# Query, key and value products as three rounded products of split weights and split latents, in a two-layer hybrid backbone on one core

## The chip, the cores and the metric

One Trainium2 chip, of which the kernel uses one core. The time is that of one execution on the device, in microseconds (us); the median of several runs counts. The core has five engines that run side by side and wait for each other by semaphores: TensorE (PE in the profile, its weight loads PEld), VectorE (DVE), ScalarE (ACT), GpSimd (POOL) and SyncE (SP), whose queue issues the weight transfers.

## The reference

Two trunk layers over 128 context tokens and 256 latent tokens, 384 in all, model width 1024, everything in fp32. Cut to what matters here:

```python
h = rms_norm(x, norm1) * (1 + scale1) + shift1
conv_in, q_lat, kv_lat, k_rope, gates = split_projection(h @ w_in)   # 1024 | 256 | 128 | 32 | 2048 wide
conv_out = conv_module(conv_in, ...)      # a * sigmoid(b), depthwise conv of width 31, LayerNorm, silu, pointwise
q   = rms_norm((rms_norm(q_lat, q_lora_norm) @ w_uq).reshape(.., 8, 96), q_norm)
ckv = rms_norm(kv_lat, kv_lora_norm)
k_nope, v = split((ckv @ w_ukv).reshape(.., 8, 64 + 64))
k   = rms_norm(concat(k_nope, k_rope), k_norm)
# latent tokens: rotary on q and k, and keys and values of 128 cached tokens are appended
att = softmax(q @ k.T * 96 ** -0.5) @ v @ w_o
x   = x + gate1 * ((sigmoid(g_conv) * conv_out + sigmoid(g_att) * att) @ w_out)
x   = x + gate2 * hier_moe(rms_norm(x, norm2) * (1 + scale2) + shift2)
```

Outputs are x of both groups, and ckv and k_rope of the context tokens for each layer.

## The kernel before, in words

**Weights.** All weights come as units of 128 x 2048 fp32 (1 MB) into a ring of six slots, one after the other on SP's queue. A load waits until the unit that was in its slot six units earlier has been used. Units of one kind, `raw_unit`, are multiplied as they lie, as fp32, by `product` (L849). Others are **split** first: `make_hi` on ScalarE copies the unit into `w_hi` in the type float32r, which rounds it (the **top**, L725), and `make_lo` on VectorE subtracts the top from the unit into `w_lo` (the **rest**, L731). `split_product` (L862) then makes three rounded products, top x top, top x rest and rest x top, into the same PSUM bank. The slot is free once the rest is made; the place of top and rest is free once TensorE has gone on to its next product. Before the gates there are three places, for the gate units two, in turn. The split units stand in `SPLIT` and are numbered in the order of use; `hi(n)` and `lo(n)` in the engines' programs make top and rest of the n-th.

**Order.** Each engine has a program that is written out by hand; nothing is scheduled. For a layer the order around the change is:

1. The norm of x; the latent products (queries' latent, keys' and values' latent, rotary key: 416 columns for each of three token tiles) and glu unit 0, interleaved. The tokens `h` are split as well.
2. ScalarE squares the three latent tiles in PSUM with accumulation (L1553), takes roots (L1555, L1556), VectorE inverts them (L1939) and scales the latents out of PSUM into `cq`, `ckv` and `kr` (L1942 to L1944). ScalarE meanwhile goes on to the sigmoid of glu unit 0 (L1561), which needs another activation table.
3. Glu units 0 to 3. For each, ScalarE makes a sigmoid and the top of the unit two further on, and VectorE multiplies into `u` (L1980, L1981), adds taps of the convolution into `z` and makes the rest of that unit. One **tap** is one instruction over 128 x 399 elements (L1967); there are 4 x 31 in a layer. `CONV_GLU` and `CONV_GATES` say how many stand after each glu and gate unit. After glu unit 2 (`LATT_AFTER`), TensorE turns `cq` and `ckv` (L840), and VectorE multiplies the turned latents by the norm's gain into `cqT` and `ckvT` (L1989) and copies the cached latent behind them (L1984).
4. Queries: six half tiles of 384 columns, two chunks of 128 in depth each, raw. Keys and values: four tiles of 512 columns each, one chunk, raw. ScalarE squares every tile of queries and keys into one of two halves of `scratch` (L1575, L1583) and copies tile and values out of PSUM; VectorE reduces the squares (L2016, L2023), with one tap behind each reduction. A square waits until the reduction two before it is done.
5. Gate units 0 to 7, each with two halves of 384 columns x 8 chunks (48 matmuls), and between them units of the conditioning projection (`ada`, L873, 16 matmuls): one after each gate unit in layer 0 (two after the last), and one after every second in layer 1. In step c VectorE does its part of the norm and the rotary of queries and keys (`steps`), `CONV_GATES[c]` taps, and then a rest; ScalarE makes a sigmoid of both halves and then a top. Ahead of gate unit 7 TensorE turns the queries.
6. When all taps are done, TensorE multiplies `z` with ones for the mean of the LayerNorm (L849, 128 x 399, the **mean product**), and the keys are turned. Attention, output products and the experts (MoE) follow.

The lookahead of the gates: the rests of gate units 0 and 1 are made after glu units 2 and 3, that of gate unit c + 2 at the end of step c.

## Time and profile before

| what | value |
|---|---|
| median of 3 runs | 939.18 us (937.98 to 943.5) |
| the profiled execution | 938.33 us, of which 936.5 us is the span from first to last instruction |
| busy: PE, DVE, ACT, POOL | 903.0, 749.6, 494.5, 34.9 us |
| chain that ended last | PE 77%, DVE 14%, ACT 3%, DMA 2% |
| raw fp32 products in it | PE ps L849, 7% of the span |
| rest of a full unit, DVE L731 | 40 in 91.5 us, 2288 ns each |
| top of a full unit, ACT L725 | 44 in 84.0 us, 1909 ns each |
| granted TensorE clock | 0.994 |

The span is the time between the first and the last instruction of the profiled core; the profiled execution's own time is 1.8 us longer. Busy time is a sum over stages, so it does not say which engine is late in one. Instructions on one engine overlap at their ends: for what one costs in a row of its kind, the distance between starts is read, not its duration. The chain of waits goes back from the last instruction to whatever released each one, so an engine named there is the one that was late.

### The profile page before, as it was taken

The numbers are of one execution on the slowest core, as the hardware profiler recorded it, in microseconds if no ns is written. First come the engines' busy times: TensorE is split into PE (matmuls) and PEld (weight loads), VectorE is DVE, ScalarE is ACT, GpSimd is POOL, SyncE is SP. The second block draws the span as 40 slices with busy tenths as digits, with TensorE's granted clock in tenths as the row PEclk, the third lists the DMA queues.
The fourth block names the chain that finished last, engine by engine and source line by source line (L and its number), as shares of the span: only waits on it lengthen the run. The fifth ranks groups of instructions, "written<-read, shape, count | busy, mean of one in ns | idle before, by whom it ended". The sixth has DMA issues, their size and how long they took to land.

```text
span 936.5 us, 14465 instructions
## 1 busy us (share of the span) xinstructions
PE 903.0 (96%) x5486; PEld 759.1 (81%) x5486; DVE 749.6 (80%) x1263; ACT 494.5 (53%) x704; POOL 34.9 (4%) x60
## 2 busy tenths in 40 slices
PE   4999999999999999999999999999999999999998
PEld 3897898768888778887868969996699878888886
DVE  4589899768754899779966998996798479986995
ACT  4345522567322687647754363336653267864872
POOL 1000000040000000000000000001400000000000
PEclk9999999999999999999999999999999999999999
DMA  9953665412464799849939336431152168993971
GB/s 369 421 203 139 232 251 192 180 46 90 185 244 170 286 373 362 329 142 387 377 124 363 129 108 270 171 135 46 46 178 95 44 235 326 374 371 132 351 278 68
DMA packets 29014, 206.54 MB, mean 221 GB/s; under 512 B 3408, under 2 KB 3440, under 8 KB 4240
## 3 DMA queue, kind: packets, MB, share of 16 engines
q1 hardware_dynamic: 28656, 204.81, 57.2%
q8 instruction: 44, 0.72, 0.3%
q0 software_dynamic: 288, 0.79, 0.2%
q14 instruction: 26, 0.21, 0.1%
HBM read 203.85 MB, written 1.74 MB: 220 GB/s over the span
## 4 chain that ended last, share of the span: by engine, by line
PE 77%; DVE 14%; ACT 3%; issue 2%; DMA 2%; SPq 0%; DVEq 0%; ACTq 0%
PE ps L862 57%; PE ps L849 7%; DVE z L1967 4%; PE ps L873 3%; DVE w_lo L731 3%; PE ps L840 2%; DMA ring<-wpre 2%; PE ps L1323 2%; ACT kT L1604 1%; PE ps L1420 1%; PE ps L1421 1%; PE ps L1146 1%; ACT w_hi L725 1%; PE ps L1134 1%; DVE w_lo L736 1%
## 5 line engine op out<-in xcount | busy, mean ns | idle before, releaser
L736 DVE TENSOR_TENSOR w_lo<-ring,w_hi 128x2048 fp32r<-128x2048 f32 (+2 forms) x104 | 227.4, 2197 | 16.1 <-ACT w_hi L1714 15.0
L862 PE MATMUL ps<-h_hi,w_hi 128*128 128x384 f32 x576 | 198.7, 345 | 1.7 <-DVE x L2212 0.6
L862 PE MATMUL ps<-h_hi,w_lo 128*128 128x384 f32 x576 | 193.6, 336 | 0.0
L862 PE MATMUL ps<-h_lo,w_hi 128*128 128x384 f32 x576 | 193.4, 336 | 0.0
L1714 ACT ACTIVATE w_hi<-ring 128x2048 fp32r<-128x2048 f32 x96 | 182.7, 1914 | 12.8 <-PE ps L862 12.5
L1967 DVE SCALAR_TENSOR_TENSOR z<-u,par,z 128x399 f32<-128x399 f32 x240 | 137.2, 630 | 1.4
L862 PEld LDWEIGHTS ps<-h_hi,w_hi 128*128 128x128 f32 x576 | 108.1, 188 | 14.3 <-issue 8.6
L731 DVE TENSOR_TENSOR w_lo<-ring,w_hi 128x2048 fp32r<-128x2048 f32 x40 | 91.5, 2288 | 27.7 <-ACT w_hi L725 27.7
L862 PEld LDWEIGHTS ps<-h_lo,w_hi 128*128 128x128 f32 x576 | 108.2, 188 | 0.5 <-issue 0.5
L862 PEld LDWEIGHTS ps<-h_hi,w_lo 128*128 128x128 f32 x576 | 108.1, 188 | 0.0
L862 PE MATMUL ps<-w_hi,hg_hi 128*128 128x512 f32 x256 | 103.3, 404 | 1.5 <-DVE hg_lo L736 1.5
L725 ACT ACTIVATE w_hi<-ring 128x2048 fp32r<-128x2048 f32 x44 | 84.0, 1909 | 32.4 <-DMA ring<-wpre 16.9
L862 PE MATMUL ps<-w_hi,hg_lo 128*128 128x512 f32 x256 | 100.6, 393 | 0.0
L862 PE MATMUL ps<-w_lo,hg_hi 128*128 128x512 f32 x256 | 100.5, 393 | 0.0
L1598 ACT ACTIVATE gates<-ps 128x384 f32<-128x384 f32 x32 | 15.7, 491 | 95.6 <-PE ps L862 95.5
L862 PEld LDWEIGHTS ps<-w_hi,hg_hi 128*128 128x128 f32 x256 | 48.1, 188 | 11.4 <-issue 1.9
L862 PEld LDWEIGHTS ps<-w_hi,hg_lo 128*128 128x128 f32 x256 | 48.1, 188 | 10.9
L862 PEld LDWEIGHTS ps<-w_lo,hg_hi 128*128 128x128 f32 x256 | 48.2, 188 | 9.3
L862 PE MATMUL ps<-w_hi,hT_hi 128*128 128x512 f32 x128 | 51.5, 402 | 0.3
L873 PE MATMUL ps<-ring,condp 128*32 128x256 f32 x768 | 51.3, 395 | 0.2 <-DMA ring<-wpre 0.2
L862 PE MATMUL ps<-w_lo,hT_hi 128*128 128x512 f32 x128 | 50.5, 395 | 0.0
L862 PE MATMUL ps<-w_hi,hT_lo 128*128 128x512 f32 x128 | 50.3, 393 | 0.0
(267 smaller groups left out, 1359.1 us busy)
## 6 DMA issues: line engine op xcount, KB each, us to landing
ring<-wpre SPq DMA_DIRECT2D x96, 1024.0 KB, 6.9
ring<-wmoe SPq DMA_DIRECT2D x96, 1024.0 KB, 6.7
x<-x SPq DMA_DIRECT2D x1, 1536.0 KB, 7.6
x_out<-x SPq DMA_DIRECT2D x4, 384.0 KB, 2.3
par<-par_in POOLq DMA_DIRECT2D x2, 304.5 KB, 7.1
const<-const_in SPq DMA_DIRECT2D x1, 314.0 KB, 2.8
ckv_out<-ckvT POOLq DMA_DIRECT2D x2, 64.0 KB, 5.3
kr_out<-kr POOLq DMA_DIRECT2D x2, 16.0 KB, 5.8
```

The lines of the kernel that those rows point to most:

```text
L725: nc.scalar.activation(w_hi[place_of(n)], slot(pre_slot(l, at)), ACT.Copy).then_inc(split_hi, 1)
L731: nc.vector.tensor_tensor(w_lo[place_of(n)], slot(pre_slot(l, PRE_AT[l][SPLIT[n]])), w_hi[place_of(n)].bitcast(F32), ALU.subtract).then_in ...
L736: return nc.vector.tensor_tensor(out, whole, leading.bitcast(F32), ALU.subtract)
L840: m = nc.tensor.transpose(out[:, n * P:(n + 1) * P], src, ident)
L849: m = mm(out, lhs[i], rhs[i], start=(i == 0), stop=(i == n - 1))
L862: m = mm(out, a, b, start=(start and i == 0 and j == 0), stop=(stop and i == n - 1 and j == 2))
L873: m = mm(ps[32 * j:32 * j + 32, ADA_BANK, 0:ADA_COLS], condp[:, 2 * j + c, at:at + 32], w[:, 2 * j + c, :], start=(u == 0 and c == 0), sto ...
L1134: m = nc.tensor.transpose(out[:, b * P:(b + 1) * P], probs[i % PROBS][:, b * P:(b + 1) * P], ident)
L1323: m = mm(out, src[:, t, f * P:(f + 1) * P], pick[:, t, :], start=(opens and c + t + part == 0), stop=(closes and c + t + part == 1 + TT))
L1598: af(gates[:, c, :], ps_of("gate", c)[:, 0:TOK], ACT.Sigmoid).then_inc(taken["act"], 1)
L1714: af(w_hi[m % MOE_PLACES], slot(moe_slot(l, m)), ACT.Copy).then_inc(split_hi, 1)
L1967: m = stt(z[:, c, :], src, dw[:, c, tap:tap + 1], z[:, c, :], ALU.mult, ALU.add)
```

## The change

The query unit `uq` and the key-value unit `ukv` become split units (1536 and 1024 of 2048 columns are converted). The turned latents are split as well, into `cqT_hi`, `cqT_lo`, `ckvT_hi`, `ckvT_lo`, which lie where the gates are written later. TensorE makes three rounded products for each of the former raw ones. With two more split units, `SPLIT` numbers gate unit 0 as 8 where it was 6. ScalarE scales the raw latents, in place of VectorE, and takes the latent banks. Six taps that stood one behind each query reduction now stand behind the last gate unit, which has 21 for 15.

```diff
-SPLIT = [e for e in PRE[0] if e[0] in ("lat", "glu", "gate", "wo", "pw2", "wout")]
+SPLIT = [e for e in PRE[0] if e[0] in ("lat", "glu", "uq", "ukv", "gate", "wo", "pw2", "wout")]
...
+def unit_width(n):
+    return {"uq": 2 * H * QK, "ukv": H * (NOPE + VD)}.get(SPLIT[n][0], UNIT)
...
-CONV_GATES = [12, 8, 11, 8, 10, 5, 15, 15]
+CONV_GATES = [12, 8, 11, 8, 10, 5, 15, 21]
...
@@ TensorE @@
-                w = raw_unit("uq", 0)
+                w = split_unit("uq", 0, 2, H * QK)
...
-                    product(out[:, 0:n], [cqT[:, c, t * P:(t + 1) * P] for c in range(2)],
-                            [w[:, c * H * QK + half * n:c * H * QK + (half + 1) * n] for c in range(2)]
-                            ).then_inc(psum_full, 1)
-                held.append(raw_used)
-                w = raw_unit("ukv", 0)
+                    split_product(out[:, 0:n], pairs(cqT_hi, cqT_lo, 2, t * P, (t + 1) * P), w(half * n, (half + 1) * n)
+                                  ).then_inc(psum_full, 1)
+                held.append(split_used)
+                w = split_unit("ukv", 0, 1, H * (NOPE + VD))
                 for t in range(KT):
+                    if t == KT - 1:
+                        pe.wait_ge(cache_split, l + 1)
...
-                        product(out[:, 0:512], [ckvT[:, t * P:(t + 1) * P]], [w[:, half * 512:(half + 1) * 512]]
-                                ).then_inc(psum_full, 1)
-                held.append(raw_used)
+                        split_product(out[:, 0:512], [(ckvT_hi[:, t * P:(t + 1) * P], ckvT_lo[:, t * P:(t + 1) * P])],
+                                      w(half * 512, (half + 1) * 512)).then_inc(psum_full, 1)
+                held.append(split_used)
@@ ScalarE @@
+                act.wait_ge(lat_inverted, l + 1)
+                for t in range(TT):
+                    src = ps_of("lat", t)
+                    af(cq[:, t, :], src[:, 0:QL], ACT.Identity, scale=lat_r[:, t:t + 1])
+                    af(ckv[:, t, :], src[:, QL:QL + KVL], ACT.Identity, scale=lat_r[:, 3 + t:4 + t])
+                    af(kr[:, t, :], src[:, QL + KVL:QL + KVL + ROPE], ACT.Copy).then_inc(taken["act"], 1)
                 for c in range(KC):
...
+                    if c == LATT_AFTER:
+                        for n in range(3):
+                            wait_full(act, l, "latT", n)
+                            src = ps_of("latT", n)[:, 0:TOK]
+                            if n < 2:
+                                af(cqT_hi[:, n, :], src, ACT.Identity, scale=pf("q_lora")[:, n:n + 1]).then_inc(lat_hi_done, 1)
+                            else:
+                                af(ckvT, src[:, 0:CTX], ACT.Identity, scale=pf("kv_lora"))
+                                af(ckvT_hi[:, TOK:KEYS], pf("cache_ckv"), ACT.Copy)
+                                af(ckvT_hi[:, 0:TOK], src, ACT.Identity, scale=pf("kv_lora")).then_inc(lat_hi_done, 1)
...
+                hi(8)
                 for t in range(KT):
...
+                hi(9)
                 act.wait_ge(head_summed, l + 1)
...
-                    if c % 2 and 8 + c // 2 < EARLY_SPLITS:
-                        hi(8 + c // 2)
+                    if c % 2 and 10 + c // 2 < EARLY_SPLITS:
+                        hi(10 + c // 2)
@@ VectorE @@
-                chain(nc.vector.reciprocal(lat_r, lat_r))
-                for t in range(TT):
-                    src = ps_of("lat", t)
-                    vs(cq[:, t, :], src[:, 0:QL], lat_r[:, t:t + 1], None, ALU.mult)
-                    vs(ckv[:, t, :], src[:, QL:QL + KVL], lat_r[:, 3 + t:4 + t], None, ALU.mult)
-                    copy(kr[:, t, :], src[:, QL + KVL:QL + KVL + ROPE]).then_inc(taken["dve"], 1)
+                nc.vector.reciprocal(lat_r, lat_r).then_inc(lat_inverted, 1)
...
                     if c == LATT_AFTER:
-                        mark(copy(ckvT[:, TOK:KEYS], pf("cache_ckv")))
+                        conv_taps(c + 1, LATT_TAPS)
                         for n in range(3):
-                            wait_full(dve, l, "latT", n)
+                            dve.wait_ge(lat_hi_done, l * 3 + (n + 1))
                             part = pf("q_lora")[:, n:n + 1] if n < 2 else pf("kv_lora")
-                            dst = cqT[:, n, :] if n < 2 else ckvT[:, 0:TOK]
-                            vs(dst, ps_of("latT", n)[:, 0:TOK], part, None, ALU.mult).then_inc(taken["dve"], 1)
-                    conv_taps(c + 1, CONV_GLU[c])
+                            dst, top = (cqT_lo[:, n, :], cqT_hi[:, n, :]) if n < 2 else (ckvT_lo[:, 0:TOK], ckvT_hi[:, 0:TOK])
+                            stt(dst, ps_of("latT", n)[:, 0:TOK], part, top.bitcast(F32), ALU.mult, ALU.subtract
+                                ).then_inc(taken["dve"], 1)
+                        lower(ckvT_lo[:, TOK:KEYS], pf("cache_ckv"), ckvT_hi[:, TOK:KEYS]).then_inc(cache_split, 1)
+                    conv_taps(c + 1, CONV_GLU[c] - (LATT_TAPS if c == LATT_AFTER else 0))
                     lo(4 + c)
...
-                    conv_taps(KC, 1)
+                lo(8)
                 for t in range(KT):
...
-                    if 8 + c < EARLY_SPLITS:
-                        lo(8 + c)
+                    if 9 + c < EARLY_SPLITS:
+                        lo(9 + c)
```

Three places of the programs, before and after. In these rows `w_hi_85`, `w_hi_86` and `w_hi_89` are the three places of tops, `w_lo_87`, `w_lo_88` and `w_lo_90` those of rests. The lines of the changed kernel have other numbers.

ScalarE between the roots of the latent norm and the sigmoid of glu unit 0, before:

```order
L1555 ACTIVATE small<-small,eps 128x3
L1556 ACTIVATE small<-small,eps 128x3
L1561 ACT_TABLE_LOAD
L1561 ACTIVATE sig<-ps 128x384
L725 ACTIVATE w_hi_86<-ring 128x2048
```

and in the changed kernel:

```order
L1573 ACTIVATE small<-small,eps 128x3
L1577 ACTIVATE cq<-ps,small 128x256
L1578 ACTIVATE ckv<-ps,small 128x128
L1579 ACTIVATE kr<-ps 128x32
L1577 ACTIVATE cq<-ps,small 128x256
L1578 ACTIVATE ckv<-ps,small 128x128
L1579 ACTIVATE kr<-ps 128x32
L1577 ACTIVATE cq<-ps,small 128x256
L1578 ACTIVATE ckv<-ps,small 128x128
L1579 ACTIVATE kr<-ps 128x32
L1584 ACT_TABLE_LOAD
L1584 ACTIVATE sig<-ps 128x384
```

Nine instructions came to stand between the roots and the table load; the first of them waits for VectorE's reciprocal.

VectorE from the last key reductions into the gate steps, before (the rest of gate units 0 and 1 is made ahead of this piece; `w_lo_87` here is that of unit 2, `w_lo_88` that of unit 3):

```order
L2023 TENSOR_REDUCE small<-scratch 128x8
L1967 SCALAR_TENSOR_TENSOR z<-u,par,z 128x399
L2029 TENSOR_TENSOR small<-small 128x32
L1967 SCALAR_TENSOR_TENSOR z<-u,par,z 128x399 x12
L731 TENSOR_TENSOR w_lo_87<-ring,w_hi_85 128x2048
L2034 RECIPROCAL small<-small 128x56
L2036 TENSOR_TENSOR q<-q,small 128x768 x3
L1967 SCALAR_TENSOR_TENSOR z<-u,par,z 128x399 x8
L731 TENSOR_TENSOR w_lo_88<-ring,w_hi_86 128x2048
```

and in the changed kernel, where the first row is the rest of gate unit 0 and the last that of gate unit 1:

```order
L747 TENSOR_TENSOR w_lo_87<-ring,w_hi_85 128x2048
L2055 TENSOR_REDUCE small<-scratch 128x8
L1997 SCALAR_TENSOR_TENSOR z<-u,par,z 128x399
L2055 TENSOR_REDUCE small<-scratch 128x8
L1997 SCALAR_TENSOR_TENSOR z<-u,par,z 128x399
L2055 TENSOR_REDUCE small<-scratch 128x8
L1997 SCALAR_TENSOR_TENSOR z<-u,par,z 128x399
L2055 TENSOR_REDUCE small<-scratch 128x8
L1997 SCALAR_TENSOR_TENSOR z<-u,par,z 128x399
L2061 TENSOR_TENSOR small<-small 128x32
L1997 SCALAR_TENSOR_TENSOR z<-u,par,z 128x399 x12
L747 TENSOR_TENSOR w_lo_88<-ring,w_hi_86 128x2048
```

Each gate unit's rest has moved one gate step nearer to its use.

ScalarE between queries and keys, before:

```order
L1575 ACTIVATE scratch<-ps 128x384
L1576 ACTIVATE q<-ps 128x384
L1583 ACTIVATE scratch<-ps 128x512
L1584 ACTIVATE k<-ps 128x8x64
L1587 ACTIVATE v<-ps 128x512
```

and in the changed kernel:

```order
L1608 ACTIVATE scratch<-ps 128x384
L1609 ACTIVATE q<-ps 128x384
L740 ACTIVATE w_hi_85<-ring 128x2048
L1617 ACTIVATE scratch<-ps 128x512
L1618 ACTIVATE k<-ps 128x8x64
L1621 ACTIVATE v<-ps 128x512
```

The top of gate unit 0, which stood before the queries, now stands between queries and keys; that of gate unit 1 stands behind the last values.

## Rows read from the trace of the kernel before

**Rows 1.** The page, part 1: busy us, share of the span, instructions.

```profile
PE 903.0 (96%) x5486; PEld 759.1 (81%) x5486; DVE 749.6 (80%) x1263; ACT 494.5 (53%) x704; POOL 34.9 (4%) x60
```

**Rows 2.** The chain of waits, layer 1, from 533 to 575: start, us, what.

```profile
543.91 1.00 PE ps L873 x16
544.91 14.80 PE ps L849 x40
559.72 8.50 PE ps L862 x48
...
568.63 1.91 ACT w_hi L725
```

**Rows 3.** The chain of waits, layer 1, from 605 to 640.

```profile
618.64 16.37 DVE z L1967 x30
...
635.15 2.93 PE ps L849 x8
```

**Rows 4.** The chain of waits over the whole span, layer 0.

```profile
61.38 8.53 PE ps L862 x48
...
81.43 14.80 PE ps L849 x40
96.23 8.38 PE ps L862 x48
...
162.74 2.76 PE ps L840 x24
...
175.75 2.89 PE ps L849 x8
```

**Rows 5.** Timeline of DVE, layer 0: start, us, engine, line, operation.

```profile
51.97 0.19 DVE L1939 RECIPROCAL small<-small 128x6 f32<-128x6 f32 x1 [2.55 <-ACT small L1556]
...
54.53 0.29 DVE L1980 TENSOR_TENSOR u<-ps,sig 128x128 f32<-128x128 f32 x1
...
58.93 2.29 DVE L731 TENSOR_TENSOR w_lo<-ring,w_hi 128x2048 fp32r<-128x2048 f32 x1
```

**Rows 6.** Timeline of ACT, layer 0, latent norm and first sigmoid.

```profile
50.26 0.42 ACT L1553 ACTIVATE unused<-ps 128x256 f32<-128x256 f32 x1
...
51.04 0.29 ACT L1554 ACTIVATE unused<-par 128x32 f32<-128x32 f32 x1
...
51.95 1.28 ACT L1561 ACT_TABLE_LOAD   x1
53.25 0.49 ACT L1561 ACTIVATE sig<-ps 128x384 f32<-128x384 f32 x1
53.63 1.91 ACT L725 ACTIVATE w_hi<-ring 128x2048 fp32r<-128x2048 f32 x1
```

**Rows 7.** Timeline of ACT, layer 0, keys and the turned queries.

```profile
91.32 0.60 ACT L1583 ACTIVATE scratch<-ps 128x512 f32<-128x512 f32 x1
...
97.33 1.28 ACT L1590 ACT_TABLE_LOAD   x1
...
163.24 3.85 ACT L1596 ACTIVATE qT<-ps,par 96x384 f32<-96x384 f32 x8 [0.97 <-PE ps L840]
```

**Rows 8.** Timeline of DVE, layer 0, reductions and the taps behind them.

```profile
86.66 0.55 DVE L2016 TENSOR_REDUCE small<-scratch 128x4 f32<-128x384 f32 x1
...
96.36 0.69 DVE L2023 TENSOR_REDUCE small<-scratch 128x8 f32<-128x512 f32 x1 [0.17 <-ACT scratch L1583]
...
97.61 6.63 DVE L1967 SCALAR_TENSOR_TENSOR z<-u,par,z 128x399 f32<-128x399 f32 x12
```

**Rows 9.** Timeline of DVE, layer 1, the first gate steps.

```profile
570.57 2.29 DVE L731 TENSOR_TENSOR w_lo<-ring,w_hi 128x2048 fp32r<-128x2048 f32 x1 [2.85 <-ACT w_hi L725]
572.78 0.49 DVE L2034 RECIPROCAL small<-small 128x56 f32<-128x56 f32 x1
...
582.48 0.95 DVE L2042 TENSOR_TENSOR q<-q,par 128x768 f32<-128x768 f32 x1
```

**Rows 10.** The page, part 6: transfers, KB each, median us from issue to landing.

```profile
ring<-wpre SPq DMA_DIRECT2D x96, 1024.0 KB, 6.9
```

More of the change, by code:

```diff
@@ L222 @@
 LATT_AFTER = 2
+LATT_TAPS = 4
 HROW_EARLY = 5
@@ L286, in pre_jobs @@
     for t in range(TT):
-        add("lat", t, "dve", 4 + t)
+        add("lat", t, "act", 4 + t)
     for c in range(KC):
@@ L463, in build @@
         probsT_at = work_at + 4 * 3 * TOK
-        cqT = v3(place("cqT", 2 * TOK, at=probsT_at), 2)
         ckvT_at = probsT_at + 4 * 2 * TOK
-        ckvT = place("ckvT", KEYS, at=ckvT_at)
+        cqT_hi = v3(place("cqT_hi", 2 * TOK, F32R, at=gates_at), 2)
+        cqT_lo = v3(place("cqT_lo", 2 * TOK, F32R, at=gates_at + 4 * 2 * TOK), 2)
+        ckvT_hi = place("ckvT_hi", KEYS, F32R, at=gates_at + 4 * 4 * TOK)
+        ckvT_lo = place("ckvT_lo", KEYS, F32R, at=gates_at + 4 * (4 * TOK + KEYS))
+        assert 4 * TOK + 2 * KEYS <= KD * TOK
+        ckvT = place("ckvT", CTX, at=ckvT_at)
         scratch_at = ckvT_at + 4 * KEYS
@@ L615, in build @@
         lat_rms = sem("lat_rms")
+        lat_inverted = sem("lat_inverted")
+        lat_hi_done = sem("lat_hi_done")
+        cache_split = sem("cache_split")
         squared = sem("squared")
@@ L724, in make_hi @@
                 eng.wait_ge(split_used, base + (earlier[-1] + 1))
-            nc.scalar.activation(w_hi[place_of(n)], slot(pre_slot(l, at)), ACT.Copy).then_inc(split_hi, 1)
+            used = unit_width(n)
+            nc.scalar.activation(w_hi[place_of(n)][:, 0:used], slot(pre_slot(l, at))[:, 0:used], ACT.Copy).then_inc(split_hi, 1)
         def make_lo(eng, l, base, n):
             eng.wait_ge(split_hi, base + (n + 1))
-            nc.vector.tensor_tensor(w_lo[place_of(n)], slot(pre_slot(l, PRE_AT[l][SPLIT[n]])),
-                                    w_hi[place_of(n)].bitcast(F32), ALU.subtract).then_inc(split_lo, 1)
+            used = unit_width(n)
+            nc.vector.tensor_tensor(w_lo[place_of(n)][:, 0:used], slot(pre_slot(l, PRE_AT[l][SPLIT[n]]))[:, 0:used],
+                                    w_hi[place_of(n)][:, 0:used].bitcast(F32), ALU.subtract).then_inc(split_lo, 1)
         def lower(out, whole, leading):
@@ L811, in _ @@
                 wait_taken(pool, l, "latT", 2)
-                pool.dma_start(ckv_out[l], ckvT[:, 0:CTX]).then_inc(ckv_stored, 16)
+                pool.dma_start(ckv_out[l], ckvT).then_inc(ckv_stored, 16)
                 pool.dma_start(kr_out[l], kr[:, 0, :]).then_inc(ckv_stored, 16)
```

## The prediction, made before the result was known

> **What bounds the kernel now.** I read the page first: TensorE is busy for 96% of the span [rows 1], an average over stages with different limits. So I went to the chain of waits in the second layer, where queries, keys and values are made. There it runs through TensorE alone: the first products on whole fp32 numbers (40 matmuls, 14.80 us), then gate unit 0 (8.50), and then leaves it: ScalarE makes the top of gate unit 2, VectorE its rest, and from there it stays on VectorE [rows 2] up to the last 30 convolution taps, which end at 635.0; the mean product starts at 635.15 [rows 3]. So what bounds the gate stage is VectorE in layer 1, and TensorE in layer 0, where the chain goes from the gates straight to the mean product at 175.75 [rows 4]. A saving on TensorE before the gates counts only if VectorE, which makes the rest of every weight unit, is there as early.
>
> Write T for the start of the first query product: 81.43 before in layer 0, 544.91 in layer 1 [rows 4, 2].
>
> **Step 1, the products: a gain on TensorE.** A 384-column rounded product costs 8.50/48 = 0.177 us [rows 2]; one of 512 columns I scale to 0.236. Queries: 6 half tiles x 2 chunks x 3 = 36, 6.4 us. Keys and values: 8 x 3 = 24, 5.7 us. Together 12.0 (14.8 if short products gained nothing), against 14.80: **2.8 us less** of TensorE per layer.
>
> **Step 2, the latents move to ScalarE: a loss.** Before, ScalarE loaded the sigmoid table at 51.95 while VectorE did the nine scalings, between its reciprocal (51.97) and the gating product at 54.53 [rows 5, 6]. Afterwards the scalings come ahead of the table load, and VectorE can do nothing in between but one small copy. Price: a token tile of three ACTIVATEs took 51.04 - 50.26 = 0.78 with three accumulator reads of 0.09, so 0.51 without [rows 6]; the two scaled ones carry a per-partition scale, and eight such 384-wide ones took 3.85, 0.47 each, against 0.38 between the starts at 53.25 and 53.63 [rows 6, 7], so 0.09 more: 0.68 a tile, 2.05 in all (bounds 1.5 and VectorE's own 2.3). With reciprocal and hand-overs, 0.25, the sigmoid ends 2.3 later, at 56.05, and VectorE goes on at 56.1 instead of 54.53: **1.5 late** (bounds 1.0 and 1.8). Nothing absorbs it: the rest of glu unit 2 ended at 58.93 + 2.29 = 61.22 and TensorE took it at 61.38, after ready work up to about 61.3 [rows 5, 4]. So TensorE starts glu unit 2 1.4 late in layer 0 and 1.5 in layer 1, and T becomes 82.85 and 546.4.
>
> The table load took 1.28 us and the sigmoid began 1.30 after its start [rows 6]. The Trainium skill (ScalarE: Activation LUTs, What ACT_TABLE_LOAD costs) adds a drain of some 1.38 us to every switch. By that rule, with the load now uncovered, each layer would lose 1.4 more; by the row, nothing. The trace disagrees with the rule here, so it is a small rival below.
>
> **Step 3, six more latent instructions.** ScalarE makes the tops of the turned latents after the query weights' top (about 1.8 us); VectorE meanwhile has four taps (2.4), so it should find them ready. Its own three rests replace three scalings. Cost nothing while those taps cover it; without them up to 1.8. Query and key-value weights are split at 3/4 and 1/2 of a 2.20 us unit, in the places where gate units 0 and 1 were split. All needed units were asked for long before: the queries' by the release of glu unit 1's slot, the others by TensorE's first product of glu unit 2 and the end of its rest.
>
> **Step 4, from T to gate unit 1: the decisive wait.** Before, VectorE began the first reduction at 86.66, T + 5.2 [rows 8]. Now the split before it is half as long (-1.1) and the gating product need not wait for a full-size split (-0.45): T + 3.7. ScalarE then goes at its own pace, since no tap stands between reductions: third square at T + 4.3, four queries x 0.77, done at T + 7.4. Now comes the new top of gate unit 0 (1.91 [rows 6]), T + 9.35; then four key/value tiles, 97.33 - 91.32 = 6.0 [rows 7]. VectorE makes gate unit 0's rest (2.2), T + 11.55, then four reductions (0.60 apart from the tap, 0.55 each tap), T + 16.2. Before it was at 97.61 - 81.43 = T + 16.2 too [rows 8]: **VectorE has been relieved of six taps and of half a split, and yet is no earlier, because ScalarE's order holds it**. Then twelve taps (6.6 us for 12 [rows 8]) and only then the rest of gate unit 1, T + 22.8 to T + 25.1. ScalarE's top of it (T + 15.4 to 17.3) is no limit.
>
> TensorE wants it at T + 12.0 + 8.5 (gate unit 0) + 1.0 (one conditioning unit in layer 0 only [rows 2]): T + 21.5 and T + 20.5. Before, gate units 0 and 1 had both been split before the reductions, and the twelve taps stood ahead of unit 2. So there is a new wait of TensorE: **3.7 us in layer 0, 4.7 in layer 1**. It eats the gain of step 1 whole: a TensorE that gained nothing would merely wait 2.8 less.
>
> Behind it in the queues: ScalarE's top of gate unit 2 waits for TensorE to leave unit 0 (over by then); VectorE's next things, reciprocals and query scaling, wait for roots that are long there.
>
> **Step 5, the gates.** In **layer 0** TensorE needs 9.5 a unit, VectorE's first step after it 582.48 - 572.78 = 9.7 [rows 9], so 0.2 more is lost, and from there VectorE gains on it (15 taps and a split, 10.4, stand against a gate, a conditioning unit and the 2.76 of transposes [rows 4]). The six moved taps end at about 175.9 and the mean product comes at 178.2: they are hidden. Sum: 1.4 - 2.8 + 3.7 + 0.2 = **+2.5**.
>
> In **layer 1** VectorE sets the end. It has the rest of unit 1 done at 546.4 + 25.2 = 571.6. Then, as before from 572.78 to 618.64, five steps: 45.85; then 15 taps (16.37/30 each, 8.2), one more split (2.2) and 21 taps (11.45) [rows 3, 9]: 639.3, mean product 639.45 against 635.15. TensorE would be there at 571.6 + 7 x 8.5 + 4 x 1.0 + 2.8 = 637.9. Cross-check: the work behind its wait of 2.85 at 570.57 [rows 9] grew by a split and six taps, 5.5, less that wait, plus 1.5 of step 2: **+4.2 to +4.3**. Here the six taps (3.3) are paid in full.
>
> After the mean product nothing is moved; the waits there are on the same engines in the same order, so I carry both shifts to the end.
>
> **The sum.** 2.5 + 4.3 = 6.8 us. Profiled execution 938.33 (span 936.5 and 1.8 around it): 945.1. The median of the runs, 939.18, is 0.85 above it: **946.0**.
>
> **Rivals.** (A) *Faster:* VectorE gets to gate unit 1 before TensorE, so the new wait is not there. It takes 3.7 and 4.7 us; the reductions would have to follow TensorE's key products (T + 12) and not ScalarE. Then TensorE keeps its gain: layer 0 1.4 - 2.8 = -1.4, layer 1 4.3 - 4.7 = -0.4: 939.2 - 1.8 = 937.4. For it: VectorE lost six taps from this stretch. Against: ScalarE's 1.91 us in the middle of it. Half of it (2.5 us earlier) gives 941. Chance 0.12.
> (B) *Slower:* squares and reductions take turns instead of overlapping (two scratch halves, and no tap to fill): 0.49 + 0.55 + 0.2 against 0.77, for four queries 1.9 a layer. Both ends hang on VectorE's time at gate unit 1, so all of it is paid: 946.0 + 3.8 = 949.8. It decides once a square waits for the reduction just before it. Chance 0.12.
> (C) The drain, per layer 1.4: 948.8. Chance 0.04.
> (D) The ring: gate units' slots come free a step later, and SP's queue holds all loads behind them. In layer 0 gate unit 4's load then begins at 108, when gate unit 1 is split, for use after 126, and a load takes 6.9 in the median [rows 10]. If it did bite in each gate, 950 to 960. Chance 0.04.
> (E) The products gain nothing: the time is the forecast's, as said.
>
> **Numbers.** The forecast 0.68. The range takes in (A)'s half, the bounds of steps 2 and 4 (about 1 us a layer each) and (B): 940 to 950.5. About 1% (9.4 us) is what a measurement can tell: faster than 929.8 needs more than the whole gain of TensorE with no loss, 0.02; slower than 948.6 holds most of (B), (C), (D) and the forecast's edge, 0.16; within 0.82.
>
> **What would show it.** Sigmoid of glu unit 0 about 2.3 after its old time; glu unit 2's products released by VectorE's rest, 1.4 late; query to value products 12.0 long; gate unit 1's first matmul waiting 3.7 and 4.7 us for VectorE's split, which follows twelve taps; the mean product at about 178.2 and 639.4; in layer 0 TensorE late there, in layer 1 VectorE. It is wrong if gate unit 1 does not wait, or if the later stages give any of it back.

## The result, and the profile after

| | before | after |
|---|---|---|
| median of the runs, us | 941.34 (937.98 to 944.21, 4 runs) | 952.39 (952.0 to 954.96, 4 runs) |
| ratio, with its 95% interval | | 1.0126 (1.0098 to 1.0154) |
| profiled execution, us | 938.33 | 952.0 |
| span, granted TensorE clock | 936.5, 0.994 | 950.2, 0.983 |

The kernel became slower by 1.3%. The forecast was 946.0 with a range up to 950.5; between the two profiled executions it had +6.8 us, and +13.7 was measured.

The page of after: part 1 (busy us of each engine), and from part 2 the granted clock in 40 slices.

```profile
PE 905.8 (95%) x5526; PEld 772.1 (81%) x5526; DVE 751.0 (79%) x1249; ACT 506.6 (53%) x736; POOL 35.0 (4%) x60
...
PEclk9999999999999999999999998999999979999999
```

TensorE is busy 2.8 us longer than in [rows 1], though its products got shorter. Busy time contains whatever runs at a lower clock, so this alone says that the clock has to be looked at.

The view of waits, engine PE, of after: line, whom it waited for, us in total, times, longest.

```profile
PE ps L878 <- DVE w_lo L747: 12.3, 5, 4.7
```

Before, the rest of a unit (then L731) held TensorE for 0.2 us in all. So the change made a wait of TensorE for VectorE's rests, 12.1 us more of it. Some of it takes the place of work saved, so it isn't yet a loss.

ScalarE's timeline of after, layer 0: the last latent copy, the table load, the sigmoid of glu unit 0 (start, us).

```profile
54.00 0.25 ACT L1579 ACTIVATE kr<-ps 128x32 f32<-128x32 f32 x1
54.27 1.28 ACT L1584 ACT_TABLE_LOAD   x1
55.56 0.49 ACT L1584 ACTIVATE sig<-ps 128x384 f32<-128x384 f32 x1
```

The sigmoid starts at 55.56 where it started at 53.25 [rows 6]: 2.31 later, as forecast. The load still took 1.28, and the sigmoid began 1.29 after its start. Now the load has nothing to hide behind, and there is still no drain beside it.

The chain of waits of after, whole span, read at the places of the prediction (start, us, what):

```profile
62.93 8.59 PE ps L878 x48
...
83.05 6.68 PE ps L878 x37
...
99.47 6.54 DVE z L1997 x12
106.01 2.21 DVE w_lo L747
108.27 10.27 PE ps L878 x48
...
180.14 2.89 PE ps L865 x8
...
490.23 1.11 PE ps L989 x8
...
530.78 10.16 PE ps L878 x48
...
575.42 2.21 DVE w_lo L747
577.68 11.20 PE ps L878 x48
...
646.04 2.89 PE ps L865 x8
...
783.58 5.77 PE ps L878 x24
```

The order of events is the predicted one: glu unit 2 behind the rest at 62.93; T = 83.05; twelve taps, then gate unit 1's rest, which ends at 108.22 = T + 25.2, and in layer 1 at 577.63 = T + 25.2 too. What was not predicted is the length of the row behind each wait. A gate or glu unit of 48 matmuls took 8.4 to 8.5 us in layer 0 of before [rows 4], and glu unit 2 of its layer 1 8.60; these three take 10.27, 10.16 and 11.20. TensorE's own timeline of after shows why (in brackets how long it sat idle before, and for what):

```profile
62.93 0.44 PE L878 MATMUL ps<-h_hi,w_hi 128*128 128x384 f32 x1 [1.74 <-DVE w_lo L747]
...
108.27 0.44 PE L878 MATMUL ps<-h_hi,w_hi 128*128 128x384 f32 x1 [3.65 <-DVE w_lo L747]
...
530.78 0.44 PE L878 MATMUL ps<-h_hi,w_hi 128*128 128x384 f32 x1 [1.94 <-DVE w_lo L747]
...
577.68 0.69 PE L878 MATMUL ps<-h_hi,w_hi 128*128 128x384 f32 x1 [4.75 <-DVE w_lo L747]
578.16 0.52 PE L878 MATMUL ps<-h_lo,w_hi 128*128 128x384 f32 x1
578.48 0.52 PE L878 MATMUL ps<-h_hi,w_lo 128*128 128x384 f32 x1
...
584.00 0.34 PE L878 MATMUL ps<-h_hi,w_hi 128*128 128x384 f32 x1
584.18 0.34 PE L878 MATMUL ps<-h_lo,w_hi 128*128 128x384 f32 x1
...
770.26 3.64 PE L889 MATMUL ps<-ring,condp 128*32 128x256 f32 x32
```

The waits are 3.65 us at gate unit 1 in layer 0 and 4.75 in layer 1, for 3.7 and 4.7 forecast. Behind the latter the matmuls start 0.32 apart, and by 584 0.18 apart. The granted clock was at its lower level (1.2 of 2.4 GHz, here called half clock) for 6.8 us there, from 576.3 on, that is from within the wait. Behind the wait of 1.74 at 62.93 it did not fall (8.59 us for the 48), behind that of 1.94 at 530.78 it did. The last row lies at the head of layer 1's experts, behind no long wait: 32 matmuls of a conditioning unit. TensorE's timeline of before has the same 32:

```profile
758.41 1.93 PE L873 MATMUL ps<-ring,condp 128*32 128x256 f32 x32
```

The view of windows of after (bounds, us, busy of PE, PEld, DVE, ACT, POOL, granted clock, DMA share, GB/s) shows the same:

```profile
100.00:120.00 20.00, 16.35 (x104) 14.61 (x103) 19.97 (x30) 7.92 (x11) 0.00 (x0) 0.91 0.28 106
520.00:540.00 20.00, 18.06 (x106) 17.16 (x105) 15.06 (x22) 7.96 (x14) 0.00 (x0) 0.91 0.29 106
560.00:580.00 20.00, 15.26 (x75) 13.92 (x74) 18.34 (x28) 15.25 (x22) 0.00 (x0) 0.91 0.31 107
760.00:780.00 20.00, 18.53 (x150) 13.42 (x150) 12.45 (x56) 9.99 (x13) 0.00 (x0) 0.74 0.52 197
```

The same view of before:

```profile
100.00:120.00 20.00, 20.00 (x135) 18.34 (x134) 17.00 (x23) 6.72 (x8) 0.00 (x0) 1.00 0.73 281
300.00:320.00 20.00, 17.80 (x170) 14.42 (x160) 16.24 (x60) 11.14 (x17) 0.59 (x1) 0.91 0.66 256
740.00:760.00 20.00, 20.00 (x161) 15.36 (x159) 10.43 (x45) 6.18 (x13) 0.00 (x0) 0.91 0.15 54
```

Before, the gate stages ran at 1.00, and the lower level came at the start (20), at the very end (935) and at the head of the experts, in both layers (0.91, one stretch of 3.4 us each, at 303 and at 754). After, there are further stretches behind the new waits (109, 532, 576.3). At the head of the experts it is 3.4 us again in layer 0 (317), but 10.2 us in layer 1 (764 to 774).

What TensorE did just before 754 in the kernel before is not a wait. Its timeline:

```profile
753.48 0.82 PE L1271 MATMUL ps<-par,xa 128*128 128x20 f32 x6
754.14 2.09 PE L840 MATMUL ps<-const,xa 128*128 128x128 f32 x9
```

The clock fell at 754.2, at the end of 28 matmuls of only 20 columns or 1 column that had run without a gap from 751.0 on. In layer 0 it fell at 303.5, near the end of the same 28. The short waits of this stage (0.55 us at 760.89 and 0.92 at 762.45) come later. In layer 1 of after it fell at 764.2, among the same matmuls.

By stage, differences of chain landmarks against before (175.75, 635.15 [rows 4, 3], and 486.09 and 770.02 for the start of layer 1's stream and of its expert products, from before's chain):

| landmark | forecast | measured | excess over forecast, of this stage |
|---|---|---|---|
| mean product, layer 0 | +2.5 | 180.14, +4.4 | 1.9 |
| start of layer 1 (L989) | +2.5 | 490.23, +4.1 | -0.25 |
| mean product, layer 1 | +6.8 | 646.04, +10.9 | 2.45 |
| first expert products, layer 1 | +6.8 | 783.58, +13.6 | 2.7 |
| end | +6.8 | +13.7 | 0.1 |

### The profile page after: what moved, and what is told of

Same layout as the page of the kernel before. It is cut to its first block, busy times and chain, and to the rows that moved or that the text cites. A ratio compares the mean times of both kernels' runs of the same rounds, so it can differ in the third digit from the quotient of the medians.

```text
span 950.2 us, 14573 instructions
## 1 busy us (share of the span) xinstructions
PE 905.8 (95%) x5526; PEld 772.1 (81%) x5526; DVE 751.0 (79%) x1249; ACT 506.6 (53%) x736; POOL 35.0 (4%) x60
## 3 DMA queue, kind: packets, MB, share of 16 engines
HBM read 203.85 MB, written 1.74 MB: 216 GB/s over the span
## 4 chain that ended last, share of the span: by engine, by line
PE 79%; DVE 12%; ACT 4%; issue 2%; DMA 2%; SPq 0%; DVEq 0%; ACTq 0%
PE ps L878 61%; PE ps L889 4%; PE ps L865 3%; DVE w_lo L747 3%; PE ps L856 3%; DVE z L1997 2%; PE ps L1340 2%; DMA ring<-wpre 2%; ACT w_hi L740 1%; ACT kT L1639 1%; PE ps L1437 1%; PE ps L1438 1%; PE ps L1163 1%; DVE w_lo L752 1%; PE ps L1151 1%
## 5 line engine op out<-in xcount | busy, mean ns | idle before, releaser
L752 DVE TENSOR_TENSOR w_lo<-ring,w_hi 128x2048 fp32r<-128x2048 f32 (+2 forms) x104 | 227.3, 2197 | 16.6 <-ACT w_hi L1749 15.6
L878 PE MATMUL ps<-h_hi,w_hi 128*128 128x384 f32 x576 | 200.6, 348 | 13.7 <-DVE w_lo L747 12.3
L878 PE MATMUL ps<-h_lo,w_hi 128*128 128x384 f32 x576 | 195.8, 340 | 0.0
L878 PE MATMUL ps<-h_hi,w_lo 128*128 128x384 f32 x576 | 195.7, 340 | 0.0
L1749 ACT ACTIVATE w_hi<-ring 128x2048 fp32r<-128x2048 f32 x96 | 182.7, 1914 | 12.9 <-PE ps L878 12.6
L747 DVE TENSOR_TENSOR w_lo<-ring,w_hi 128x2048 fp32r<-128x2048 f32 (+2 forms) x44 | 97.4, 2213 | 23.5 <-ACT w_hi L740 23.5
L740 ACT ACTIVATE w_hi<-ring 128x2048 fp32r<-128x2048 f32 (+2 forms) x48 | 89.3, 1860 | 36.9 <-DMA ring<-wpre 17.0
L878 PEld LDWEIGHTS ps<-w_hi,hg_lo 128*128 128x128 f32 x256 | 48.1, 188 | 10.9
```

What stands on the lines that cost most here:

```text
L740: nc.scalar.activation(w_hi[place_of(n)][:, 0:used], slot(pre_slot(l, at))[:, 0:used], ACT.Copy).then_inc(split_hi, 1)
L747: nc.vector.tensor_tensor(w_lo[place_of(n)][:, 0:used], slot(pre_slot(l, PRE_AT[l][SPLIT[n]]))[:, 0:used], w_hi[place_of(n)][:, 0:used].bi ...
L752: return nc.vector.tensor_tensor(out, whole, leading.bitcast(F32), ALU.subtract)
L878: m = mm(out, a, b, start=(start and i == 0 and j == 0), stop=(stop and i == n - 1 and j == 2))
L1749: af(w_hi[m % MOE_PLACES], slot(moe_slot(l, m)), ACT.Copy).then_inc(split_hi, 1)
```

## Experiments

The theory after the result, called N: the new waits at the gates are as predicted, and on top of them comes half clock, which makes the missing 6.9 us. Its rivals: L, that the loss lies with the latents' scalings on ScalarE, and P, that it lies with the products, which are made on TensorE's path.

The runs came in four groups: 1, 2, 4 and 5; 3, 6, 7 and 8; 9 and 10; 11. All runs of one group shared their chip and the runs of before (medians 940.3 to 940.8). After itself was measured ahead of them, next to 941.3 for before, so against after I go by the ratios to before, and by the rows. One kernel's runs spread by some 7 us, and the granted clock goes with the spread: in the second group runs of before at 0.994 took 937.9 to 938.2, those at 0.984 to 0.985 took 944 to 945.2, some 6 us for each 0.01. So a median is compared with a median, and a landmark with a landmark.

**1. Gate unit 1's rest ahead of the taps.** In after, the rest is made first in gate step 0, and nine of that step's taps go behind the last gate unit.

```diff
-CONV_GATES = [12, 8, 11, 8, 10, 5, 15, 21]
+CONV_GATES = [3, 8, 11, 8, 10, 5, 15, 30]
...
+                    if c == 0:
+                        lo(9)
                     conv_taps(KC, CONV_GATES[c])
...
-                    if 9 + c < EARLY_SPLITS:
+                    if 0 < c and 9 + c < EARLY_SPLITS:
```

> The changed kernel with the rest of gate unit 1 made ahead of the taps of gate step 0, and nine of those twelve taps moved behind the last gate unit, so that the rest of gate unit 2 is not late either. Theory N (the new wait: gate unit 1's rest stands behind twelve taps, TensorE waits 3.9 us in layer 0 and more in layer 1, and runs at half clock, 1.2 GHz, for some 3.4 us after each wait): no wait at gate unit 1, no stretch at half clock there; layer 0 ends its gates some 3.1 us earlier (VectorE's taps are then last, at about 177), layer 1 within 1 us of where it did (VectorE is last there too); 949.3, with 3 us either way for where the later stretches at half clock fall. Rival L (the loss comes from the latent scalings on ScalarE and what follows them): unchanged, 952.

Measured: 954.43 us (953.38 to 954.87), 1.014 (1.0108 to 1.0171), no better than after. Chain of this kernel:

```profile
177.55 4.42 PE ps L865 x8
...
645.61 5.02 PE ps L865 x8
```

Windows of this kernel:

```profile
640.00:660.00 20.00, 13.73 (x67) 9.31 (x62) 12.86 (x30) 8.60 (x19) 1.41 (x4) 0.83 0.16 53
760.00:780.00 20.00, 18.53 (x129) 12.79 (x128) 10.73 (x55) 8.51 (x12) 0.00 (x0) 0.65 0.46 163
```

The waits at gate unit 1 went, and both mean products started earlier than after's, by 2.6 and 0.4 us, as expected. But the moved taps made a wait at another place: TensorE now waited for `z` ahead of them (7.4 us in two waits, 5.4 the longest), ran them at half clock (4.42 and 5.02 instead of 2.89), and the heads of the experts spent 6.8 and 17.1 us at half clock instead of 3.4 and 10.2. So a wait moved is not a wait removed. The value expected, 949.3, had no term for half clock behind the new waits, only a margin of 3 us. One row goes against a fixed price: glu unit 2 of layer 1 waited 1.94 here too, and the clock stayed at 1.00 behind it (window 520 to 540).

**2. The scalings back on VectorE.** In after, the nine latent scalings return to where before had them (the lines of the diff ahead of the prediction, reversed).

> The changed kernel with the nine latent scalings back on VectorE, ahead of the first gating product, as in the kernel before. Theory N plus the sizes of the trace: glu unit 2 starts 1.4 us earlier in layer 0 and 1.8 in layer 1, and with no wait ahead of it in layer 1 the half-clock stretch there (1.6 us lost) is gone; the waits at gate unit 1 stay as they are, 3.9 and more; 947.2. Rival L: the whole loss goes, 941.

Measured: 949.1 (948.85 to 950.83), 1.0093 (1.006 to 1.0125): 3.3 us less than after by the medians, though the two intervals overlap. Glu unit 2 of layer 1 takes 8.59 again, and from the layer's start to its mean product it is 151.7 us, where after had 155.8; TensorE's wait for the rests falls from 12.3 to 8.7 us. The waits at gate unit 1 stay (3.80 and 4.75), with their half clock (11.37 and 10.20 us for the 48 matmuls). The expected value for N was 947.2; the other, 941, lies outside the interval and falls.

**3. The scalings on ScalarE in before, alone.** The same move, made in the kernel before.

> The kernel before with one part of the change alone: the nine latent scalings on ScalarE. Glu unit 2 starts 1.4 us late in layer 0 and 1.8 in layer 1, and with a wait of that length there is half clock behind it in layer 1, 1.6 more: 938.3 + 4.8 = 943.1. If the scalings were free on ScalarE: 938.3.

Measured: 945.7 (942.09 to 950.82, 10 runs), 1.0047 (1.0026 to 1.0068), against 945.1 expected from the median of before. In layer 1 glu unit 2 took 10.21 us at 532.40. By the chain of its profiled execution (the slowest of the ten) layer 0 reached its mean product 2.1 later than in before, and layer 1 took 152.3 from its start to its own, for 149.1. So step 2 by itself costs some 5 us, where the prediction had 2.9: 1.6 of the difference is the clock at glu unit 2.

**4. The six taps back behind the query reductions.** In after, `conv_taps(KC, 1)` after each query reduction, and 15 taps behind the last gate unit.

> The changed kernel with the six taps back behind the query reductions. As I put it in the prediction (six taps paid in full in layer 1, where VectorE is last) the time would fall by 3.3 - 0.6 = 2.7, to 949.3. By the trace after, TensorE with its half-clock stretch is 0.5 us later than VectorE in layer 1, so the taps are covered and the taps between the reductions only delay gate unit 1's rest by 0.6 in each layer: 952 to 953.

Measured: 950.17 (949.51 to 952.75), 1.0104 (1.0069 to 1.0139). Chain, and one window, of this kernel:

```profile
181.43 2.88 PE ps L865 x8
...
647.63 2.89 PE ps L865 x8
```

```profile
760.00:780.00 20.00, 17.57 (x160) 13.50 (x159) 14.14 (x56) 9.97 (x14) 0.00 (x0) 0.91 0.60 218
```

Both mean products come later than in after, not earlier. The profiled execution was shorter all the same (950.45 for 952.0), because the head of the experts of layer 1 had one stretch of 3.4 us at half clock and not 10.2; by the intervals the two kernels are not told apart. So the prediction's "here the six taps (3.3) are paid in full" falls: in layer 1 of after VectorE's last tap ended at 645.2, and TensorE came to the mean product at 646.04 from its own work. The value that the prediction's step gave, 949.3, is near the median, but not for its reason.

**5. Two products instead of three.** In after, `split_product` is called with `made=2` for queries, keys and values: rest x top is left out, so the output is less exact and TensorE has some 4.0 us less work a layer.

> The changed kernel with two of the three products for queries, keys and values; rest x top is left out, so the outputs are less exact. TensorE has 20 matmuls less in a layer, 4.0 us. Theory N: VectorE's time for gate unit 1's rest does not depend on TensorE, which waits 4 us longer: 952, with the time of the products worth nothing; a longer wait may bring more half clock. Rival P (TensorE's rate is what counts, and three short products are too slow): 944 to 948.

Measured: 950.57 (947.54 to 955.4), 1.0103 (1.0052 to 1.0153). Chain of this kernel:

```profile
577.45 11.21 PE ps L878 x48
...
646.19 2.88 PE ps L865 x8
```

Gate unit 1 (108.14 and 577.45) and both mean products (180.01 and 646.19) start within 0.25 us of after's, so a saving of 4.0 us on TensorE is worth nothing here, as rival (E) said. It was not all spent in the wait at gate unit 1, which was 2.12 and 3.85 us: TensorE first waited 2.06 us for ScalarE's copies of the keys in each layer (at 93.49 and 562.80), and each of these waits had 3.4 us at half clock behind it. It is the rows that speak against P; the time by itself doesn't, since P's 944 to 948 reaches into the measured interval.

**6. The same wait in before.** In before, gate unit 1's rest is made behind 20 taps of gate step 0 (none in step 1), so that TensorE waits for it there, and nothing else is changed.

```diff
-CONV_GATES = [12, 8, 11, 8, 10, 5, 15, 15]
+CONV_GATES = [20, 0, 11, 8, 10, 5, 15, 15]
...
-                    lo(4 + c)
+                    if c < KC - 1:
+                        lo(4 + c)
...
+                    if c == 0:
+                        lo(7)
```

> The kernel before (raw products, scalings on VectorE) with one thing moved: the rest of gate unit 1 is made in gate step 0 behind twenty taps, twelve of that step and the eight of step 1. VectorE then has it at T + 27.1 (T is the first query product), TensorE wants it at T + 24.3 in layer 0 and T + 23.3 in layer 1: a wait of 2.8 and 3.8 us and no other change. Theory N with the clock (TensorE runs at half clock for a stretch after such a wait): layer 0 loses 2.8 + 1.7, layer 1 ends its gates 4.9 later than before (VectorE has slack there): 938.3 + 9.4 = 947.7, and rows show half clock at gate unit 1. If the stretches at half clock came at fixed places and not after waits: 944.3, with none there.

Measured: 958.48 (954.37 to 960.02), 1.0189 (1.0153 to 1.0225). Chain and windows of this kernel:

```profile
98.37 10.90 DVE z L1967 x20
582.60 11.50 PE ps L862 x48
```

```profile
100.00:120.00 20.00, 15.09 (x81) 14.19 (x80) 16.79 (x24) 4.51 (x5) 0.00 (x0) 0.83 0.62 240
580.00:600.00 20.00, 17.40 (x92) 16.57 (x93) 11.31 (x10) 5.30 (x5) 0.00 (x0) 0.83 0.33 111
```

I had sized the waits too small: they were 4.9 and 5.8 us for 2.8 and 3.8 expected, and the time is 11 us above the 947.7 expected. But what the run is for, it shows: in the places where before has a clock of 1.00, a wait alone brings half clock with it, for 6.8 us each, and the 48 matmuls take 11.5 where they took 8.5. The price of such a wait here is its length plus some 3 us.

**7. The waits filled.** In after, TensorE multiplies 20 times into the free bank ahead of gate unit 1 and 7 times ahead of glu unit 2, in both layers. Nothing reads these products.

```diff
+                def fill(name, index, n):
+                    out = begin(name, index)
+                    for _ in range(n):
+                        mm(out[:, 0:TOK], h_hi[:, 0, 0:P], h_hi[:, 0, :], start=True, stop=True)
```

> The changed kernel with TensorE kept busy in its two waits: 20 matmuls of 128 x 384 ahead of gate unit 1 (3.6 us) and 7 ahead of glu unit 2 (1.2 us), whose results nothing reads; each is shorter than the wait, so nothing is late by them. Theory N with the clock: the waits end where they did, but no half clock follows: 1.7 us less in layer 0, 1.6 less before the queries of layer 1, and 0.5 at its gates: 948.2, give or take 3 for the later stretches. If half clock did not depend on the idle time: 952.

Measured: 949.32 (947.66 to 951.28, 5 runs), 1.0083 (1.0051 to 1.0115). TensorE's timeline of this kernel at gate unit 1, layer 0:

```profile
104.78 3.75 PE L1071 MATMUL ps<-h_hi 128*128 128x384 f32 x20
108.66 0.44 PE L879 MATMUL ps<-h_hi,w_hi 128*128 128x384 f32 x1
```

Its windows:

```profile
100.00:120.00 20.00, 19.87 (x132) 17.85 (x131) 19.97 (x29) 9.41 (x11) 0.00 (x0) 1.00 0.32 111
520.00:540.00 20.00, 19.49 (x122) 18.34 (x121) 14.10 (x24) 9.37 (x24) 0.00 (x0) 1.00 0.28 106
760.00:780.00 20.00, 18.50 (x144) 13.69 (x143) 14.26 (x56) 9.39 (x12) 0.00 (x0) 0.66 0.65 217
```

The waits end about when they did (gate unit 1 at 108.66, after 108.27), and TensorE does more work. The clock stays at 1.00 at all three places (two of them in the fence; 1.00 from 560 to 600 too), and the units take 8.75 (gate unit 1, layer 0) and 8.59 (glu unit 2, layer 1). Layer 0 reaches its mean product 1.0 us earlier than after (179.10), and layer 1 takes 153.6 from its start to its own, for 155.8: 3.3 us gained in these stages, where N had 3.8. The medians differ by 3.1 us, but the intervals just overlap (up to 1.0115 here, from 1.0098 on for after). This is the other half of run 6: what is lost behind a wait is lost by the clock. In its profiled execution the head of the experts had 13.7 us at half clock in both layers (after: 3.4 and 10.2), and that execution took 951.28, the longest of the five.

**8. All three undone or mended.** After, with the rest ahead of three taps as in run 1, the scalings on VectorE, the six taps back, and 24 taps behind the last gate unit.

> The changed kernel with three edits together: rest of gate unit 1 ahead of the taps of step 0 (nine of its twelve taps go to the end), scalings back on VectorE, six taps back behind the query reductions. By the same replay layer 0 ends its gates 2.4 us earlier than the kernel before (TensorE and VectorE nearly level at 173.3), layer 1 1.1 later (VectorE last): 938.3 - 1.3 = 937.0, and level with or just below the kernel before. Where TensorE waits for the last taps, the mean product may run at half clock, 1.5 more for each layer: 940.

Measured: 941.99 (938.64 to 946.4, 12 runs), 1.0013 (0.9992 to 1.0033). Gate unit 1 follows unit 0 without a wait (103.64, 8.53 us) and layer 0's mean product comes at 173.8, 2.0 before [rows 4]: here the shorter products do pay. In layer 1 it starts at 634.18, 1.0 before [rows 3] (from the start of the layer 150.2 us, for 149.1 in before), but takes 4.61 us behind a wait of 2.1 for the taps. The landmarks are the expected ones; the median is 2 us above the upper of the two values expected, the profiled execution (939.06) below it.

**9. First taps of glu units 1 to 3 on ScalarE.** Run 8, with ScalarE making the first product of `z` of these chunks (an activation with scale and bias), three instructions less for VectorE.

> The kernel of the three edits, and the first taps of glu units 1 to 3 (a scale and a bias) on ScalarE, which is idle there; VectorE does a tap of an older chunk meanwhile. Theory N (in layer 1 VectorE's sum of work sets the end of the gates): VectorE has 3 x 0.49 = 1.5 us less in each layer, layer 1 ends its gates 1.5 earlier, layer 0, where TensorE is last, does not change: 942.0 - 1.5 = 940.5, and 1 less if the mean product no longer runs at half clock. Rival (the end of the gates is set by ScalarE's order and VectorE only follows): 942.

Measured: 941.19 (938.12 to 945.19, 12 runs), 1.0003 (0.9984 to 1.0023). The mean product of layer 1 came at 634.36 with that layer begun 0.7 later, so some 0.5 of about 1.5 us was gained. VectorE's wait for ScalarE's tops stayed at 22.6 us: it was relieved where it was waiting anyway. TensorE's timeline of this kernel at that mean product:

```profile
634.36 2.93 PE L866 MATMUL ps<-z,const 128*128 128x399 f32 x8 [2.00 <-DVE z L2004]
```

It waited 2.00 us for the taps, nearly as long as in run 8, and this time the clock did not fall.

**10. Three idle products ahead of layer 1's mean.** Run 9, with three matmuls that nothing reads while TensorE waits for the last taps.

> The same with three matmuls of 128 x 384 (0.5 us) that nothing reads, ahead of the mean product of layer 1, where TensorE still waits 0.6 for the last taps. Theory N with the clock: no half clock at that mean product, 939.5 to 940.5. If it makes no difference, the same as without them.

Measured: 940.23 (935.87 to 942.35, 12 runs), 0.9992 (0.9974 to 1.0011). The mean product takes 2.95 us. But run 9 had 2.93 without the three matmuls, so this pair doesn't show that they kept the clock up. The wait that they were to fill was 2.0 us in run 9's trace and not 0.6.

**11. Five taps earlier.** Run 10, with the time freed in run 9 used: one tap more in each glu step from 1 on and two ahead of gate unit 1's rest, 19 behind the last gate unit for 24.

```diff
-CONV_GATES = [3, 8, 11, 8, 10, 5, 15, 24]
+CONV_GATES = [3, 8, 11, 8, 10, 5, 15, 19]
...
+                        conv_taps(KC, 2)
                         lo(9)
```

> The kernel with three edits, first taps on ScalarE and the three filling matmuls, in which VectorE now does five taps earlier: three in the glu steps, in the time that ScalarE took over, and two ahead of the rest of gate unit 1, whose top ScalarE has ready about 1 us after VectorE gets there. The run with the first taps on ScalarE showed 0.4 us gained where I expected 1.5: the time saved fell into VectorE's waits for ScalarE. If that reading is right, five taps fewer behind the last gate unit end layer 1's gates 2.7 us earlier, and TensorE is nearly level with VectorE there: 940.2 - 2.7 = 937.5. If taps anywhere cost the same, 940.

Measured: 938.28 (937.31 to 941.88, 12 runs), 0.9977 (0.9956 to 0.9999) against 940.76 for before in the same group.

TensorE's wait for the taps is gone (1.3 us in run 10), its waits for the rests are 2.7 us in all (2.1 in run 10), and the clock was 0.995 in the profiled run. Yet the mean product of layer 1 comes 149.4 us after the start of its layer, where run 10 had 149.6: 0.2 of the 2.7 expected, because TensorE now comes there from its own work. The profiled execution of run 10 had 10.2 us at half clock at the head of layer 0's experts, this one 3.4, so most of the difference between the two medians may be clock; their intervals overlap. It is the fastest version made here, but its interval barely ends below 1.

## Why the prediction failed

**What held.** Step 1: query to value products took 11.9 us (82.98 to 94.87 on TensorE's timeline of after), 12.0 forecast. Step 2: the sigmoid 2.31 later (2.3), glu unit 2 of layer 0 1.55 late (1.4), T = 83.05 (82.85). Step 4: the reductions done at T + 16.4 (16.2), gate unit 1's rest at T + 25.2 (25.1) in both layers, after twelve taps, with waits of 3.65 (3.7) and 4.75 (4.7). Rival (E), that products gain nothing and the time is the same, is what run 5 shows. Rivals (A) to (D) did not occur: the wait is there, the reductions were done at T + 16.4 where (B) had T + 18.1, there is no drain, and ScalarE's waits for the ring were 17.0 us in all, 16.9 before.

**What failed.** Steps 2 and 4 price a wait of TensorE by its length, and the sum adds only these. Runs 6 and 7 show a second term: behind such a wait TensorE runs at half clock. Worked out from after's rows: 10.27 - 8.5 = 1.75 at gate unit 1 of layer 0; 10.16 - 8.60 = 1.6 at glu unit 2 of layer 1; 11.20 - 8.5 = 2.7 at gate unit 1 of layer 1, of which VectorE's lateness covers all but some 0.7 (its last tap ended at 645.2, TensorE came at 646.0). With 0.3 because glu unit 2 of layer 1 was 1.8 late for 1.5, that is some 4.3 us; the landmarks have 4.1 of the 6.9 us up to there.

The rest stands in the sentence "After the mean product nothing is moved; ... so I carry both shifts to the end". The work is indeed unmoved, but the head of layer 1's experts took 2.7 us longer on the same instructions, 1.7 of it on the 32 matmuls of a conditioning unit (3.64 where before had 1.93), at half clock. From the mean product to the first expert products of layer 1 it was 134.2 us with no half clock between them (run 6), 134.8 to 134.9 with 3.4 us of it (run 4, before), 136.2 with 6.8 (run 2) and 137.4 to 137.7 with 10.2 to 13.7 (after and runs 3, 5 and 7). So the 2.7 us go with the time at half clock; why it was 10.2 us in after, 3.4 in run 4, 17.1 in run 1 and none in run 6 is not shown. It is not simply a matter of what the gates did: run 7 had no half clock in its gates and still 13.7 us of it later. It stays open what sets it.

**Step 5, layer 1.** "VectorE sets the end", with the six taps paid in full: run 4 gave the taps back and the mean product came 0.2 us later against the start of its layer (647.63 - 491.60 against 646.04 - 490.23). TensorE, slowed by its clock, had become the later one, by some 0.7 us.

**What could have been read.** The trace of before has one wait of the size forecast, with half clock behind it, on TensorE's timeline:

```profile
20.48 0.69 PE L862 MATMUL ps<-w_hi,h_hi 128*128 128x416 f32 x1 [3.72 <-DVE h_lo L1927]
...
21.31 0.55 PE L862 MATMUL ps<-w_hi,h_lo 128*128 128x416 f32 x1
21.65 0.55 PE L862 MATMUL ps<-w_hi,h_hi 128*128 128x416 f32 x1
```

These matmuls start 0.34 apart, and 0.18 to 0.19 apart from 26.0 on; the clock was at half for 3.4 us, which is 1.7 us of work lost. Its longest wait at the gates, 1.31 us ahead of the mean product at 635.15, has a clock of 1.00 behind it. One such stretch behind each of the waits forecast would have made some 1.7 at gate unit 1 of layer 0, 1.7 at glu unit 2 of layer 1, and little at gate unit 1 of layer 1, where VectorE leads by 1.5: about 949.6, an estimate made after the event.

## What to carry to other kernels

Before you put a wait of the tensor engine into a sum, add what it costs afterwards: here waits of 1.9 to 5.8 us brought, in most cases, 1.6 to 3 us more for the same matmuls at half clock, and filling the waits with products that nobody reads gave this back. When one engine's work gets shorter, look at which engine releases its next step: here 2.8 us of shorter products, and even 4.0 more, were worth nothing until the rest of the next unit was made ahead of the taps. And relieving an engine where it waits anyway gains little: in run 9 VectorE had 1.5 us less work in a layer, and the gates of layer 1 ended 0.5 earlier.

## What was not expected of the hardware

The clock fell behind a wait of 1.94 us (glu unit 2, layer 1) and not behind one of 1.74 (layer 0) in one and the same execution, and stretches at half clock lasted 3.4 us at 109 and at 532, 6.8 at 576.3 and 10.2 at 764. Waits of 1.73 to 1.75 us at glu unit 2 of layer 0 left the clock alone in runs 1, 3, 4 and 5 as well. But waits of about 2 us are not told apart by their length: it fell behind 1.92 (runs 3, 4, 5), 2.06 (runs 1, 5), 2.10 (run 8) and 2.12 (run 5), and not behind 1.94 in run 1 and 2.00 in run 9. Nor does it take a wait: in before it fell at 303.5 and at 754.2 while TensorE ran matmuls of 1 and 20 columns one after the other, and the page counts it as busy there. In runs of one unchanged kernel the time follows the granted clock by about 6 us for each 0.01, which goes with a spread of 938 to 946 for before.

The Trainium skill (TensorE: Matmul & The Clock Gate, Part 1) has this gate, which halves the array's clock after little activity and gives it back once the array is kept busy; the rows behind the waits agree. It also puts the penalty of that ramp at under 1% of a typical kernel's span. Here the excess over the forecast was 6.9 of 950 us, 0.7%, and half of what the change cost. All stretches at half clock of after together are 32 us, of before 14; at half speed that is at most 16 us or 1.7% of the span for after, so for all of them together under 1% is not shown.
